# Two transformer-like blocks in one kernel: six small moves in the order of work and in what it waits for

## What is computed

```python
# block 1
proj = rmsnorm(x, g) @ w_in;  q, k, v, u, g_attn, g_ssm = split(proj)
y_attn = sliding_window_attention(q, k, v, sinks, rel_bias) @ w_attn_branch
z = gelu(s5_ssm(u, ...));  z = z * sigmoid(z @ w_glu);  y_ssm = z @ w_ssm_branch
merged = sigmoid(g_attn) * y_attn + sigmoid(g_ssm) * y_ssm
x = x + rmsnorm(merged @ w_out, norm_mix_post)
f = square(relu(rmsnorm(x, norm_mlp_pre) @ w_ff_in)) @ w_ff_out
x = x + rmsnorm(f, norm_mlp_post)
# block 2: the recurrence
r, i = sigmoid(u @ wa + ba), sigmoid(u @ wx + bx)
a = exp(-8 * r * softplus(-lam));  beta = sqrt(1 - a * a)
h = scan(a, beta * i * u)            # once forward, once backward
```

## Time and profile before

| | |
|---|---|
| median of three runs | 1434.8 us |
| the profiled execution's own time | 1436.06 us |
| its span, first to last instruction | 1433.9 us |
| TensorE matmul busy | 1406.4 us, 98% |
| VectorE busy | 886.2 us, 62% |
| ScalarE busy | 613.2 us, 43% |
| mean granted TensorE clock | 0.995 |

### The profile page before, as it was taken

The page is one execution under the profiler, slowest core; times in us unless marked ns, Lnnn a source line. Parts: engine busy times, 40 slices in busy tenths (PEclk is TensorE's granted clock), DMA queues, the critical chain, the costliest instruction groups (busy, mean ns, idle before and its releaser), DMA issues.

```text
span 1433.9 us, 17607 instructions
## 1 busy us (share of the span) xinstructions
PE 1406.4 (98%) x7142; PEld 1123.8 (78%) x7142; DVE 886.2 (62%) x1308; ACT 613.2 (43%) x980; POOL 10.2 (1%) x23
## 2 busy tenths in 40 slices
PE   8999999999999999999999999999999999999997
PEld 6787778788788888887787777767888888888886
DVE  7999755647636354354668888489864433443446
ACT  6474553333313222132336777788553222231232
POOL 0000000000000000000000000000000000000000
PEclk9999999999999999999999999999999999999999
DMA  5222123231333323233132222323233332233233
GB/s 201 86 75 86 63 75 131 85 107 50 102 90 102 103 89 103 88 99 105 47 103 82 59 74 67 103 67 96 88 103 103 96 106 92 88 105 101 88 89 102
DMA packets 42528, 132.67 MB, mean 93 GB/s; under 512 B 8992, under 2 KB 11296, under 8 KB 42192
## 3 DMA queue, kind: packets, MB, share of 16 engines
q1 hardware_dynamic: 40784, 125.98, 28.6%
q0 software_dynamic: 1120, 5.44, 1.3%
q10 hardware_dynamic: 544, 0.13, 0.0%
HBM read 127.34 MB, written 2.10 MB: 90 GB/s over the span
## 4 chain that ended last, share of the span: by engine, by line
PE 79%; DVE 12%; ACT 6%; issue 3%; DMA 1%; SPq 0%; DVEq 0%; ACTq 0%
PE gp L1657 22%; PE gp L1659 21%; PE gp L1658 21%; DVE w_lo L965 2%; PE mp L1863 2%; PE mp L1874 2%; PE mp L1841 2%; ACT w_hi L519 1%; PE mp L1753 1%; PE mp L1755 1%; PE mp L1754 1%; PE mp L1657 1%; PE mp L1658 1%; PE mp L1659 1%; PE gp L1753 0%
## 5 line engine op out<-in xcount | busy, mean ns | idle before, releaser
L1657 PE MATMUL gp<-h_hi,w_hi 128*128 128x512 f32 x944 | 371.8, 394 | 5.7 <-DVE w_lo L1042 2.0
L1659 PE MATMUL gp<-h_hi,w_lo 128*128 128x512 f32 x944 | 368.3, 390 | 0.0
L1658 PE MATMUL gp<-h_lo,w_hi 128*128 128x512 f32 x944 | 368.2, 390 | 0.0
L965 DVE TENSOR_TENSOR w_lo<-raw,w_hi 128x1024 fp32r<-128x1024 f32 x198 | 241.8, 1223 | 119.1 <-ACT w_hi L519 118.6
L519 ACT ACTIVATE w_hi<-raw 128x1024 fp32r<-128x1024 f32 x198 | 207.2, 1050 | 142.3 <-PE gp L1659 80.7
L1657 PE MATMUL gp<-a_hi,w_hi 128*128 128x512 f32 x652 | 256.1, 393 | 2.6 <-DVE w_lo L965 1.8
L1659 PE MATMUL gp<-a_hi,w_lo 128*128 128x512 f32 x652 | 253.8, 389 | 0.0
L1658 PE MATMUL gp<-a_lo,w_hi 128*128 128x512 f32 x652 | 253.8, 389 | 0.0
L1657 PEld LDWEIGHTS gp<-h_hi,w_hi 128*128 128x128 f32 x944 | 177.6, 188 | 53.6 <-issue 7.3
L1659 PEld LDWEIGHTS gp<-h_hi,w_lo 128*128 128x128 f32 x944 | 177.6, 188 | 37.5
L1658 PEld LDWEIGHTS gp<-h_lo,w_hi 128*128 128x128 f32 x944 | 177.7, 188 | 35.9
(11 more groups left out here) (304 smaller groups left out, 1647.0 us busy)
## 6 DMA issues: line engine op xcount, KB each, us to landing
raw<-slabs SPq DMA_DIRECT2D x198, 512.0 KB, 3.5
arena<-slabs SPq DMA_DIRECT2D x29, 512.0 KB, 3.5
arena<-x_in POOLq DMA_DIRECT2D x1, 2048.0 KB, 8.1
a_hi<-arena POOLq DMA_DIRECT2D x16, 128.0 KB, 2.2
out_t<-arena SPq DMA_DIRECT2D x8, 256.0 KB, 2.2
arena<-x_in SPq DMA_DIRECT2D x3, 512.0 KB, 6.7
arena<-bias POOLq DMA_DIRECT2D x1, 1024.0 KB, 5.5
raw<-slabs SPq DMA_DIRECT2D x12, 64.0 KB, 2.4
```

Of the source, the lines that this page charges most:

```text
L965: TT(w_lo[:, n % RING, :], raw(n), w_hi[:, n % RING, :].bitcast(F32), ALU.subtract).then_inc(w_lo_ready, 1)
L1657: pe.matmul(dst, hi, x_hi(t), start=t == 0, stop=False)
L1658: pe.matmul(dst, hi, x_lo(t), start=False, stop=False)
L1659: ins = pe.matmul(dst, lo, x_hi(t), start=False, stop=t == tiles - 1)
```

## The change

Six moves; no arithmetic is added or taken away:
1. `q` 0 is placed in bank `mp` 0 instead of a `gp` bank.
2. `turn_states` of the last chunk is issued on VectorE after `logits(0)` of attention 1.
3. `branch_s`: its first slab runs as `pair_late_tile`, that is tiles 0 to 2 of outputs 0 and 1, then tile 3 of both; `a_low` of merged chunk `m-1` is issued between the gating and the adding of chunk `m`; ScalarE's weight split is issued one copy earlier.
4. Feed-forward 1, first part: the last hidden chunk's read and the residue of chunk 6 go ahead of a weight split; the last `add_square` of the last part goes ahead of two weight splits.
5. Recurrence: sigmoids wait for the scan that reads the row which they overwrite (`lru_scanned`) and no longer for the whole chunk (`lru_free`); the tanh takes over that wait. In windows 1 and 2 one weight split is issued ahead of the roots (ScalarE) and of the first `states` (VectorE), and another on VectorE a step earlier.
6. The first gate products wait for the copied attention only from product 4 on.

```diff
@@ PLACE
+                elif _name == "q" and _k == 0:
+                    PLACE[_o] = mp, 0
@@ scalar: branch_s
+            split(SLAB["branch_s"] + AHEAD)
             for j in range(COUNT["branch_s"]):
-                split(SLAB["branch_s"] + AHEAD + j)
                 for m in (2 * j, 2 * j + 1):
                     act.wait_ge(m_val, m + 1)
                     nc.scalar.activation(a_hi[:, m, :], gate1[m], ACT.Copy, scale=0.5).then_inc(a_hi_ready, 1)
+                    if m % 2 == 0 and j + 1 < COUNT["branch_s"]:
+                        split(SLAB["branch_s"] + AHEAD + j + 1)
@@ scalar: sigmoids, tanhs
-                if t >= 2:
-                    act.wait_ge(lru_free, t - 1)
...
+                    if t >= 2:
+                        act.wait_ge(lru_scanned, 2 * (t - 2) + d + 1)
...
                 act.wait_ge(lru_sig, 8 * j + 4 * i + 4)
+                if j:
+                    act.wait_ge(lru_free, 2 * j + i - 1)
@@ scalar: windows
+                if j and not last:
+                    split(next(ahead))
                 roots(j)
                 if j:
                     merged_hi(2 * j - 2)
                     merged_hi(2 * j - 1)
-                split(next(ahead))
+                if last or not j:
+                    split(next(ahead))
@@ vector: attention 1
-                after[n_turn].append(lambda ct=ct: turn_states(ct))
+                if ct < CT - 1:
+                    after[n_turn].append(lambda ct=ct: turn_states(ct))
...
-            attention(att1, gate_slab)
+            attention(att1, gate_slab, lambda: turn_states(CT - 1))
@@ vector: branch_s
                     STT(out=tmp[m % 2], in0=gate2[m], scalar=1.0, in1=src, op0=ALU.add,
                         op1=ALU.mult).then_inc(out_read, 1)
+                    if m:
+                        merged_part(m - 1)
                     dve.wait_ge(out_read, OUT["branch_s"] + m + 1)
                     TT(gate1[m], gate1[m], tmp[m % 2], ALU.add).then_inc(m_val, 1)
-                    a_low("merged", m, gate1[m], 0.5)
+            merged_part(DC - 1)
@@ vector: feed-forward 1
-                    elif k % 2:
+                    elif k % 2 and k < FF1_PART - 1:
                         split(SLAB["ff"] + AHEAD + START + k // 2)
                     TT(tmp[k % 2], take("ff", s0 + k), R[:, :], ALU.mult).then_inc(out_read, 1)
+                    if not p and k == FF1_PART - 1:
+                        low(k - 1)
+                        split(SLAB["ff"] + AHEAD + START + k // 2)
...
+                    if last and m == DC - 1:
+                        add_square("post2", m - 1)
                     split(SLAB["ff"] + AHEAD + s0 + FF1_PART + m)
@@ vector: states
-                V.up(dve.tensor_tensor_scan(UC[:, t, :], a[:, 0, :], x[:, 0, :], 0.0, ALU.mult, ALU.add))
-                V.run(dve.tensor_tensor_scan(beta[:, 1, ::-1], a[:, 1, ::-1], x[:, 1, ::-1], 0.0, ALU.mult, ALU.add))
+                dve.tensor_tensor_scan(UC[:, t, :], a[:, 0, :], x[:, 0, :], 0.0, ALU.mult, ALU.add).then_inc(lru_scanned, 1)
+                dve.tensor_tensor_scan(beta[:, 1, ::-1], a[:, 1, ::-1], x[:, 1, ::-1], 0.0, ALU.mult,
+                                       ALU.add).then_inc(lru_scanned, 1)
+                dve.wait_ge(lru_scanned, 2 * t + 2)
@@ vector: windows
-                split(next(ahead))
+                if j != 1:
+                    split(next(ahead))
...
+                if j and not last:
+                    split(next(ahead))
                 states(j, 0)
...
-                split(next(ahead))
+                if last or not j:
+                    split(next(ahead))
                 apply_gate(*gates[2])
...
                 states(j, 1)
+                if not j:
+                    split(next(ahead))
@@ tensor
+            def pair_late_tile(name, tiles, x_hi, x_lo, ready):
+                n = SLAB[name]
+                pe.wait_ge(w_lo_ready, n + 1)
+                for some in (range(tiles - 1), (tiles - 1,)):
+                    for e in range(2):
+                        dst = bank(name, e)
+                        if some[0] == 0 and freed_by(name, e) > 0:
+                            pe.wait_ge(out_read, freed_by(name, e))
...
-            for j in range(COUNT["branch_s"]):
-                gemm("branch_s", j, 4, 2, h, hl,
-                     (lambda t: pe.wait_ge(h_lo_ready, H_AT["z2"] + t + 1)) if j == 0 else None)
+            pair_late_tile("branch_s", 4, h, hl, lambda t: pe.wait_ge(h_lo_ready, H_AT["z2"] + t + 1))
+            for j in range(1, COUNT["branch_s"]):
+                gemm("branch_s", j, 4, 2, h, hl)
...
                         pe.wait_ge(s_turned, 32 * DC)
+                    elif o == 4:
                         pe.wait_ge(at_copied, len(att2.units))
```

More of the change, by code:

```diff
@@ L297, in build @@
             sem("lru_products"), sem("lru_sigmoids"), sem("lru_tanh"), sem("lru_decay"), sem("lru_root"), sem("lru_states"))
+        lru_scanned = sem("lru_scans_done")
         gate_used = sem("gate_applied")
@@ L1320, in _, with merged_part @@
                     h_low(H_AT["z2"] + m, m, U[:, m, :])
+            def merged_part(m):
+                a_low("merged", m, gate1[m], 0.5)
             for j in range(COUNT["branch_s"]):
@@ L1403, in ff1_part @@
                         split(SLAB["q2"] + AHEAD)
-                    if last and m:
+                    if last and 0 < m < DC - 1:
                         add_square("post2", m - 1)
```

12 lines of the change are left out of this document (11 added, 1 removed).

## The result

The changed kernel took **1422.4 us** (median of 4 runs, 1421.44 to 1424.22) beside 1435.12 of the kernel before: ratio 0.9912, interval 0.99 to 0.9924, so 12.7 us faster. Forecast were 1421.0 and a gain of 13.8. A second set of 4 runs, made later, gave 1421.62 beside 1435.67, 14.05 faster. The profiled execution took 1423.08, its span is 1420.9, 13.0 less than before.

A forecast was written before the change was run, and what follows sets the result against it. TensorE's matmuls were taken to bound the kernel (1406.4 of 1433.9 us busy), so only its waits count; 0 + 1.0 + 3.15 + 3.95 + 2.5 + 3.2 = 13.8 off 1434.8 gives 1421.0 us, range 1418.8 to 1424.5.

The forecast's parts named there:

- Step 1: Query 0 in a free bank: its wait of 0.73 only moves to `turn_win(0)`, gain 0 (bounds 0 and 0.73).
- rival that the wait was truly saved: Before query 0: the wait really goes and VectorE's split comes early enough, 1420.3 us; chance 0.05.
- Step 2: Attention 1, turned states behind the first logits: TensorE's wait falls from 1.63 to about 0.65, gain 1.0 us.
- Step 3: Branches: late tile and VectorE order remove three waits (0.80, 1.21, 1.14), gain 3.15 us (bounds 2.0 and 3.15).
- Step 4: Late tile of feed-forward 1: wait of 2.06 and slow clock behind it go, gain 3.95 us (bounds 2.06 and 3.95).
- Step 5: Norm after feed-forward 1, sums ahead of splits: wait of 1.31 and slow clock go, gain 2.5 us.
- Step 6: Recurrence: four waits, for copied attention, sigmoids and `w_lo` twice, go; gain 3.2 us (bounds 0.3 and 3.2).
- rival of a chain-bound recurrence: Recurrence bound by its chain: only 0.3 of 3.2 is left, 1423.9 us; chance 0.14.
- two falls inside the kernel: Trace before: the clock falls behind idle times of 2.06 and 1.31, and not behind 1.63, 1.21, 1.14 or 1.30.
- The clock's rival: A new or kept fall of the clock, for instance before `turn_win(0)`, 1.7 us each: 1422.7 to 1424.4; chance 0.14.
- a sign of being wrong: In the changed profile, the clock falling at a new place would show the forecast wrong; no size given.
- no wait came back one place on: Opposite of the rival that each removed wait returns one place on, some 2 us left, 1433 us; chance 0.03.

The follow-up runs named there:

- Run 1: Changed kernel with query 0 put back in the bank of `k`, the five other moves kept: 1421.97 us.
- Run 9: Changed kernel with ScalarE's two sines issued earlier and the last `turn_states`' two sums put behind the second unit's scaled probabilities and weight split: 1420.15 us.
- run 4: Kernel before with the finer scan waits of the recurrence and one VectorE weight split a step earlier: 1432.78 us, ratio 0.9983.
- run 5: Kernel before with only the `branch_s` order on VectorE and ScalarE changed, its first slab as before: 1432.94 us, ratio 0.9979.
- run 6: Kernel before with nine unused matmuls filling TensorE's late-tile wait of 2.06: 1433.95 us, ratio 0.9994.
- run 2: Kernel before with only the finer scan waits for sigmoids and tanh in the recurrence, no split moved: 1435.58 us, ratio 0.9999.
- run 3: Kernel before with only the recurrence's weight splits moved, sigmoids still waiting for the whole chunk: 1432.73 us, ratio 0.9983.
- run 8: Changed kernel with ScalarE's two sines issued earlier and the last `turn_states`' two sums put behind the first scaled probabilities: 1422.13 us.

## Why the prediction held, and where it was off

- **Step 1 (0)** held in size and in place: 1.09 before `turn_win(0)` (forecast about 1.0), 11.54 to query 1 as before. Run 1 shows it. The rival that the wait was truly saved is refuted.
- **Step 2 (1.0)** held: measured 0.89, with the spread told above. As forecast, VectorE's own work sets it, and not ScalarE's exponentials, done at 148.2. `inverse_sums` was put at 148.25, with the 1.51 of the start 149.76:

```profile
149.82 0.17 DVE L1266 TENSOR_TENSOR arena<-arena 128x4 f32<-128x4 f32 x1
```

  The wait left is 0.85 where 0.65 was forecast, partly because TensorE came there 0.11 sooner. Run 9 takes this wait away, by moving the two sums that stand ahead of `inverse_sums`, and gains 0.93 more.
- **Step 3 (3.15)** was mis-sized: 3.79. The mechanism and both halves held (3.17 for VectorE's order, 0.62 for the late tile, where 2.35 and 0.80 were forecast), but the forecast added printed idle times, and a wait costs more. The row counts idle time from the end of the last matmul, 0.39 after its start, while at full cadence the next one starts after 0.227: 0.16 for each wait. The second matmul behind it then came 0.31 to 0.34 behind the first, some 0.1 late. Three waits with 0.25 each make 0.75, of which the wait of 0.19 that is left takes some back.
- **Step 4 (3.95)** held: 3.96, and the stage takes 10.88, forecast 10.9. Of it 1.6 is the clock, which the kernel before does not lose in every execution (run 4), so for the median the sum was too high here. In the eight traces with moves 2 to 6 the clock did not fall there once, nor at the norm of step 5.
- **Step 5 (2.5)**: 2.62, and 680.88 - 671.63 = 9.25 from `first_squares` to the next stage, forecast 9.2. With the same wait of 1.31, the next stage began 686.58 - 677.20 = 9.38 later in run 5 and 9.37 later in run 6, against 10.40 before. The clock did not fall there in these two traces, and did before and in those of runs 2, 3 and 4. So the move is worth 1.6 in any case and 1.0 more in the executions in which the clock would have fallen.
- **Step 6 (3.2)** held as a sum, 3.52, for a reason that I had only half. I gave the waits for sigmoids and for `w_lo` separate prices; run 2 shows that the first alone is worth 0.86, since VectorE is full and the wait moves on to the split, and runs 3 and 4 that the splits free it. The times on the way were good to 0.3: with the 9.75 gained before, the second sigmoids of windows 2 and 3 ended at 966.7 and 992.3 (forecast 966.8 and 992.1), and stage out2 began at 1004.46 + 9.75 = 1014.2 (forecast 1017.74 - 3.2 = 1014.5). Against the rival of a chain-bound recurrence stand run 3 and the 3.52 itself.
- **The clock.** The forecast's reading that the trace before shows two falls inside the kernel is wrong: it shows a third, at 10 to 13 us, behind a wait of 2.04 (the last section has the rows). The clock's rival came true in part: the clock fell at 25 us, which the prediction had named as a sign of being wrong, behind a wait that exists in both kernels and not before `turn_win(0)`.
- **The sum.** By the traces the five priced steps brought 14.8, 1.0 more than forecast, mostly in step 3. Against it stand falls of the clock that the sum had left out: the 1.6 and 1.0 that the kernel before doesn't always lose, and the 1.5 at the start that the changed kernel sometimes does. Medians 12.7 and 14.05 faster lie on either side of 13.8. That they are so near is partly luck, since the two errors have opposite signs.

That no wait came back one place on, but for move 1's, was the bet of the forecast. The moves for which I had worked out the next deadline paid; run 8 is the same kind of bet lost, because I checked the unit that waited and not the next one.

## What to carry to other kernels

Before a wait is removed, ask what the releasing engine does in the microseconds ahead: if it is full there, earlier inputs may not bring its later products forward, and most of the wait moves on (run 2; in run 8 all of it did). Then the instruction that TensorE needs must itself be moved ahead, or work that nobody needs yet moved out of the full stretch into an idle one (runs 4 and 9). Price a stall by the distance of two starts, not by its printed idle time; here that was 0.25 more for each, and 1.0 to 1.6 more where the clock fell behind it, as it did in four of six and four of five traces. A fall seen in one trace is not yet a part of the price: look at a second one.

## What the runs showed of the hardware

The clock's fall behind a wait is not a fixed part of its price. The late tile's wait of 2.06 was followed by seven or eight matmuls spaced at 0.427 in four of the five traces in which it stood unfilled; they began 0.5 to 1.5 us behind its end, and in the fifth trace there were none. The norm's wait of 1.31 with eight single-column matmuls behind it brought a fall in four of six traces. The first norm's wait with sixteen of them brought one in the four traces where it was 0.65 to 0.95, and none in the other ten, where it was 0.40 at most. A wait of 2.0 to 2.9 at 8 us, with matmuls of 128x512 behind it, was followed by slow matmuls in 13 of the 14 traces. In the kernel before (the wait, then the clock, 0.50, behind it):

```profile
8.27 0.47 PE L1657 MATMUL gp<-h_hi,w_hi 128*128 128x512 f32 x1 [2.04 <-DVE w_lo L1042]
```

```profile
10.00:13.00 3.00, 2.77 (x7) 2.20 (x8) 3.00 (x6) 3.00 (x5) 0.00 (x0) 0.50 1.02 404
```

Waits of 1.63, 1.30, 1.21 and 1.14 brought none; behind the first stand transposes, behind the second products of 64x512, behind the last two matmuls of 128x512. The Trainium skill, "TensorE: Matmul & The Clock Gate", Part 1, says that the gate's window runs freely; a fall that comes and goes behind the same wait agrees with it. Its cost by the rows is 0.2 for each slow matmul, and by the stretches 0.8 to 2.4 per fall. One kernel's runs differ by 4 us, and low clocks go with long spans: over the 27 runs of the kernel before that stood beside runs 1 to 3 and 5, spans went from 1431.6 at a mean clock of 0.997 to 1435.7 at 0.993.

Nine unused matmuls in a wait of 2.06 cost nothing: they ended at 378.49, the tile behind them started at 378.50, and from the first late tile to there it took 6.29, for 6.30 before.
